# Two mixer layers: where the recurrence's reciprocal, its square root and half of a convolution stand between the attention steps

## The reference

```
q, k, v, lx, lg, sb, sc, sx = jnp.split(proj, offs, axis=-1)
y_attn = sliding_window_attention(q, k, v, sinks)
lx = causal_depthwise_conv(lx, lru_conv_w, lru_conv_b)
y_lru = jax.nn.gelu(lg) * rg_lru(lx, lru_gate_a_w, lru_gate_a_b, lru_gate_x_w, lru_gate_x_b, lru_lambda)
y_sc = sb * causal_depthwise_conv(sc * sx, sc_conv_w)
y = jnp.concatenate([y_attn, y_lru, y_sc], axis=-1)
return y @ w_out
```

```
log_a = -LRU_C * r * softplus(-lam);  a = exp(log_a)
mult = sqrt(-expm1(2.0 * log_a));     mult = 1 at the first token
h_t = a_t * h_{t-1} + mult_t * (i_t * x_t)
```

## Time and profile before

| | us |
|---|---|
| median of 3 runs | 3105.79 |
| lowest, highest | 3105.39, 3108.03 |
| the profiled execution's own time | 3100.99 |
| its span, first to last instruction | 3099.2 |
| PE busy in the span | 2965.0 (96%) |
| DVE busy | 1647.5 (53%) |
| ACT busy | 1150.1 (37%) |

### The profile page before, as it was taken

The page is one execution under the profiler, slowest core; times in us unless marked ns, Lnnn a source line. Parts: engine busy times, 40 slices in busy tenths (PEclk is TensorE's granted clock), DMA queues, the critical chain, the costliest instruction groups (busy, mean ns, idle before and its releaser), DMA issues. The chain is left out here.

```text
span 3099.2 us, 38755 instructions
## 1 busy us (share of the span) xinstructions
PE 2965.0 (96%) x13952; PEld 2308.7 (74%) x13952; DVE 1647.5 (53%) x1771; ACT 1150.1 (37%) x1355; POOL 260.0 (8%) x425
## 2 busy tenths in 40 slices
PE   6998898999999998999999999999999999999998
PEld 4886565767676767888877688887888877778886
DVE  6745846666666657555256565523555246543322
ACT  4124634666666653222235322213222135432211
POOL 0110002222222220000000000000000000000000
PEclk9989999999999999999999999999999999999999
DMA  7552226999999996554222154422554222122221
GB/s 283 170 180 99 82 110 252 359 358 360 371 350 350 357 322 243 190 189 149 95 86 81 56 201 179 175 95 82 203 189 163 95 98 69 68 95 95 95 95 68
DMA packets 115276, 554.59 MB, mean 179 GB/s; under 512 B 20593, under 2 KB 22130, under 8 KB 72946
## 3 DMA queue, kind: packets, MB, share of 16 engines
q1 hardware_dynamic: 88690, 490.39, 43.0%
q0 software_dynamic: 26496, 62.96, 5.8%
HBM read 548.06 MB, written 37.75 MB: 189 GB/s over the span
## 5 line engine op out<-in xcount | busy, mean ns | idle before, releaser
L181 ACT ACTIVATE stream_high<-stream_raw 128x2048 fp32r<-128x2048 f32 x151 | 289.2, 1916 | 801.4 <-PE ffn_ps_psum L571 756.7
L186 DVE TENSOR_TENSOR stream_low<-stream_raw,stream_high 128x2048 fp32r<-128x2048 f32 x156 | 356.7, 2287 | 410.8 <-ACT stream_high L181 410.3
L569 PE MATMUL ffn_ps_psum<-h_high_f,stream_high 128*128 128x512 f32 x1344 | 525.0, 391 | 0.0
L571 PE MATMUL ffn_ps_psum<-h_high_f,stream_low 128*128 128x512 f32 x1344 | 523.1, 389 | 0.0
L570 PE MATMUL ffn_ps_psum<-h_low_f,stream_high 128*128 128x512 f32 x1344 | 522.9, 389 | 0.0
L324 DVE TENSOR_TENSOR expert_low<-expert_raw,expert_high 128x2048 fp32r<-128x2048 f32 x128 | 293.4, 2292 | 222.4 <-ACT expert_high L320 218.9
L571 PEld LDWEIGHTS ffn_ps_psum<-h_high_f,stream_low 128*128 128x128 f32 x1344 | 252.3, 188 | 53.0
L570 PEld LDWEIGHTS ffn_ps_psum<-h_low_f,stream_high 128*128 128x128 f32 x1344 | 252.4, 188 | 52.3 <-issue 0.2
L569 PEld LDWEIGHTS ffn_ps_psum<-h_high_f,stream_high 128*128 128x128 f32 x1344 | 252.4, 188 | 51.9 <-issue 0.2
L320 ACT ACTIVATE expert_high<-expert_raw 128x2048 fp32r<-128x2048 f32 x128 | 244.2, 1909 | 118.1 <-PE experts_g_psum L571 112.2
L803 DVE TENSOR_TENSOR ffn_sg<-ffn_sg,ffn_ps_psum 128x512 f32<-128x512 f32 x88 | 60.6, 688 | 419.4 <-PE ffn_ps_psum L571 410.8
(11 more groups left out here) (490 smaller groups left out, 4561.7 us busy)
## 6 DMA issues: line engine op xcount, KB each, us to landing
expert_raw<-in_exp_gu SPq DMA_DIRECT2D x128, 1024.0 KB, 9.7
stream_raw<-in_ffn_gu SPq DMA_DIRECT2D x88, 1024.0 KB, 4.9
expert_raw<-in_exp_dn SPq DMA_DIRECT2D x64, 1024.0 KB, 7.1
con<-in_w_mod SPq DMA_DIRECT2D x120, 512.0 KB, 5.4
stream_raw<-in_ffn_dn SPq DMA_DIRECT2D x44, 1024.0 KB, 4.9
mix_mod_rows<-in_w_ada POOLq DMA_DIRECT2D x32, 512.0 KB, 4.6
stream_raw<-in_w_in SPq DMA_DIRECT2D x16, 1024.0 KB, 4.9
pieces_raw<-in_w_in SPq DMA_DIRECT2D x13, 1024.0 KB, 6.0
```

What stands on the lines that cost most here:

```text
L181: self.nc.scalar.activation(self.high[:, q], self.raw[:, q], ACT.Copy).then_inc(self.high_done, 1)
L186: self.nc.vector.tensor_tensor(self.low[:, q], self.raw[:, q], self.high[:, q].bitcast(F32), ALU.subtract)\
L569: mm(out, w[0], x[0], start=start, stop=False)
L571: return mm(out, w[1], x[0], start=False, stop=stop)
```

## The change

Four edits, all in `second_mixer`, so each acts twice in an execution.

1. The reciprocal of 1 - t is taken in two halves of 128x512. The first stays ahead of the first item; the second stands behind `scale(0)`.
2. The product with -2t and the floor, which need both halves, move from ahead of the first item to behind `find_top(1)`.
3. ScalarE takes the root as exp(0.5 ln x) in place of Sqrt: two passes over 128x1024, in the set that holds both, which is loaded behind `split(6)` of item 1. The two passes stand behind the evacuation of item 2. The multiplication into i moves on VectorE from item 2 to item 3.
4. The convolution's second half moves from ahead of `scale(7)` to behind it.

```diff
@@ ScalarE @@
                             split(6)
-                            act.wait_ge(mult_in, 1)
-                            a(flat(xc), flat(xc), ACT.Sqrt).then_inc(rooted, 1)
+                            nc.scalar.preload_act_table_set(LOG_EXP)
                         elif i:
                             evacuate(FIRST + i)
+                        if i == 2:
+                            act.wait_ge(mult_in, 1)
+                            a(flat(xc), flat(xc), ACT.Ln).then_inc(rooted, 1)
+                            act.wait_ge(rooted, 1)
+                            a(flat(xc), flat(xc), ACT.Exp, scale=0.5).then_inc(rooted, 1)
@@ VectorE @@
+                    def convolve(n):
+                        x, y = proj[:, 10 + n, :], proj[:, 12 + n, :]
+                        chain(v.tensor_scalar(y, x, w3(2, n), None, ALU.mult))
+                        for k in range(2):
+                            d = 2 - k
+                            chain(v.scalar_tensor_tensor(out=y[:, d:], in0=x[:, 0:S - d], scalar=w3(k, n), in1=y[:, d:],
+                                                         op0=ALU.mult, op1=ALU.add))
...
-                    chain(v.reciprocal(flat(xc), flat(xc)))
-                    chain(v.scalar_tensor_tensor(out=flat(xc), in0=flat(th), scalar=-2.0, in1=flat(xc), op0=ALU.mult, op1=ALU.mult))
-                    v.tensor_scalar(flat(xc), flat(xc), 1e-30, None, ALU.max).then_inc(mult_in, 1)
+                    chain(v.reciprocal(xc[:, 0, :], xc[:, 0, :]))
...
+                        if i == 1:
+                            chain(v.scalar_tensor_tensor(out=flat(xc), in0=flat(th), scalar=-2.0, in1=flat(xc), op0=ALU.mult, op1=ALU.mult))
+                            v.tensor_scalar(flat(xc), flat(xc), 1e-30, None, ALU.max).then_inc(mult_in, 1)
                         if i == 2:
                             split(6)
-                            dve.wait_ge(rooted, 1)
+                        if i == 3:
+                            dve.wait_ge(rooted, 2)
                             chain(v.memset(xc[:, :, 0:1], 1.0))
                             chain(v.tensor_tensor(flat(i_), flat(i_), flat(xc), ALU.mult))
-                        if i == 3:
                             dve.wait_ge(decay_done, 1)
...
-                            for n in range(2):
...
+                            convolve(0)
                         scale(i)
+                        if i == 0:
+
+                            chain(v.reciprocal(xc[:, 1, :], xc[:, 1, :]))
+                    convolve(1)
```

## The result

| | before | changed |
|---|---|---|
| median of 4 runs, us | 3106.47 | 3087.20 |
| lowest, highest | 3105.39, 3108.03 | 3084.29, 3091.34 |
| ratio (95% interval) | | 0.9943 (0.9928 to 0.9958) |
| span of the profiled execution | 3099.2 | 3089.5 |

The forecast was 3095.6, in a range from 3090.5 to 3101.0. Yet the spans of the profiled executions differ by 9.7 us. Which of the two is the change's own effect is what the experiments were for.

What follows compares the result with a forecast made beforehand. PE, busy 96% of the span, bounds the kernel; only its waits for `scale` in the mixers (14.8 us) can be won. 3.04 + 2.09 = 5.13 a mixer, 10.2 used for two: 3105.79 - 10.2 = 3095.6 us, range 3090.5 to 3101.0.

Steps and rivals of the forecast that it cites:

- `turn(0)` 3.6 gained: First mixer, item 0: with the reciprocal halved, TensorE no longer waits ahead of turn(0); 3.6 us gained, 1.1 in hand.
- wait of 0.3 left at `turn(2)`: First mixer, item 2: about 0.3 us still waited, turn(2) 4.57 us earlier, as root and one load leave ScalarE's stretch.
- new wait of 1.5 at `turn(3)`: Ln and Exp hold out_to_high(0), and so find_top(3); TensorE waits 1.5 us where it had not, leaving 3.04 gained.
- 0.54 left at `turn(7)`: Convolution's second half moved behind scale(7) brings turn(7) 2.09 us forward; 0.54 of its 2.63 us wait stays.
- half a reciprocal 3.35: VectorE's reciprocal of 512 elements, read off the line through other sizes: 3350 ns, bounds 0.35 and 6.55 us.
- 5.13 a mixer: Gain for one mixer: 3.04 us up to turn(3) plus 2.09 from the convolution; 10.3 for two.
- the sum's last: Gain of 10.2 us from both mixers, taken off the runs' median 3105.79 to give 3095.6.
- A half as dear as a whole: Rival: each half reciprocal takes 6.55 us, so 1.8 us slower in all, 3107.6; chance 0.05.
- loads on the path: Rival: Ln and Exp, or the loads before exponents(2), cost 2.57 us more; gain only 5.1, 3100.7; chance 0.13.
- a gain given back: Rival: TensorE comes earlier but loses it behind the mixer, at weights or stage ends; no change, 3105.8; chance 0.08.
- no new wait: Rival: the two passes do not hold turn(3), so its 1.5 us goes too; 3 us more, 3092.5; chance 0.08.
- a drain behind each load: Skill's rule, rejected: about 1380 ns drain per table load, 2.66 us a switch; turn(2) would come 2.76 us later.

Runs made afterwards that it cites:

- filled: Kernel before, with products that write nothing read put into TensorE's waits ahead of turn(0), turn(2) and turn(7) of each mixer: 3103.5 ± 0.8 us, ratios 1.0005 and 0.9994.
- the Sqrt kernel: Changed kernel with one Sqrt pass in place of Ln and Exp, at the same new place, no table set named: 3090.4 us, ratio to before 0.9956.

## Why the prediction missed

- **Terms of the sum.** `turn(0)` 3.6 gained, wait of 0.3 left at `turn(2)` (0.22), new wait of 1.5 at `turn(3)` (1.53), 0.54 left at `turn(7)` (0.53), half a reciprocal 3.35 (3.354), a pass 1.06 (1.05, 1.06), 5.13 a mixer (175.9 - 170.8 = 5.1). All are right, and so is the path on which they were found. The rest fell by 10.8 ± 0.6 against 10.2.
- **The step that failed** is the sum's last: "I use 10.2 ... and I carry the gain over to it". It priced a wait by its own length and took the clock as given: the clock stood in the sum at nothing, without a reason. The loss fell too, by 5.2 ± 1.3, and by this the time is 16.1 lower in the means and not 10.2. About 2 of the 5.2 (2.3 ± 1.0) is what filling the waits took back as well. For the other 3 (44.3 ± 0.9 filled, 41.4 ± 1.2 changed) no experiment shows a cause. The profiles have it at the starts of parts, four dips in each of the two filled ones, none, two and none in the changed ones; whether the place in time decides there, or chance, is open.
- **The range** ended 5.1 us below the forecast, with no case for the clock, and went by the spread of three runs; eleven of one kernel spread over 14 us. The first comparison was besides a lucky one: four runs at 3087.5 in the mean, where fifteen give 3089.2 ± 1.2. That, too, is below 3090.5, but by hardly more than one standard error.
- **The rivals.** A half as dear as a whole, loads on the path, a gain given back, and "no new wait" are all refuted, by the profile after and by the rest, which fell by the whole 10. So is the rule of a drain behind each load: in the Sqrt kernel the pass began 0.01 behind the end of its load (1678.50 + 1.28 to 1679.79), so the Trainium skill's 2.66 us for a switch (ScalarE: Activation LUTs, "What ACT_TABLE_LOAD costs") shows here as 1.28.

## What to carry to other kernels

Follow a wait back to the instruction that ends it, and move what needs no answer soon from ahead of it to behind it: that alone gave all of the 10 us that were worked out. A removed wait can be worth more than its length: in one execution the 3.54 us ahead of `turn(0)` was followed by half clock that cost another 2.4. So let the range reach beyond the sum on that side. For half a per cent, take the clock from several runs and several comparisons, not from one profile, and look at loss and rest beside the time, never in place of it.

## What the runs showed of the hardware

- A half-clock stretch takes 1.6 to 1.7 us of time where TensorE sets the pace (first mixer of the kernel before 177.5, with one, against the second's 175.9, with none), and nothing where VectorE does (12.84 us from `turn(3)` to `turn(4)` with and without one).
- The same wait of 3.54 us in the same kernel was followed by half clock in one execution and not in another, and one of 2.6 us in one mixer and not in the other. Waits of 0.2 to 1.5 us in the changed kernel's three profiles never were.
- Waits of up to 6.7 us, seven in the profile where eight were expected, raised the loss by 12.3 ± 1.3; products through them took it all back, but not the time.
- Reciprocals of 4, 32, 512 and 1024 elements (178, 353, 3350 and 6553 ns) lie on one line: 6.25 ns an element, some 0.15 us fixed.
